# Experts of a mixture: gate and up products as three products of f16 parts, with weights scaled and split one expert ahead

## What is computed

```python
cap = max(1, EC_CAPACITY * N // N_EXPERTS)
aff = jax.nn.softmax((xt @ w_router).astype(jnp.float32), axis=-1)
gates, idx = lax.top_k(aff.T, cap)
xs = xt[idx]
h = jax.nn.silu(jnp.einsum('ecd,edf->ecf', xs, w_gate)) * jnp.einsum('ecd,edf->ecf', xs, w_up)
y = jnp.einsum('ecf,efd->ecd', h, w_down) * gates[..., None].astype(x.dtype)
out = jnp.zeros((N, D), x.dtype).at[idx.reshape(-1)].add(y.reshape(-1, D).astype(x.dtype))
```

## Time and profile before

| | us |
|---|---|
| median of 3 runs | 3354.52 |
| lowest, highest | 3351.68, 3358.54 |
| the profiled execution | 3351.22 |
| its span | 3349.4 |

### The profile page before, as it was taken

How to read it: one execution, slowest core, us unless ns; L and a number is a source line. 1 busy time by engine, 2 the same in 40 slices (tenths; PEclk the granted TensorE clock), 3 DMA queues, 4 the chain that set the end, 5 groups by cost and what they waited for, 6 DMA issues and landing times. The chain is left out here.

```text
span 3349.4 us, 39224 instructions
## 1 busy us (share of the span) xinstructions
PE 2938.2 (88%) x14279; PEld 1610.0 (48%) x14279; DVE 1591.5 (48%) x2416; ACT 1308.5 (39%) x2322; POOL 1002.2 (30%) x928
## 2 busy tenths in 40 slices
PE   7999999869999999779868969999009999999998
PEld 4555555535555555423222324454006566566664
DVE  3244444358888888565575543332781111111111
ACT  3333333249999999674345422222001110110100
POOL 0111111148888888650163001111000111111111
PEclk9999999979999999899979979999559999999999
DMA  5112232225111111288858973433403645556551
GB/s 150 40 52 79 79 91 77 68 68 199 33 33 33 33 33 33 67 358 294 282 198 329 308 239 115 134 113 94 161 29 104 188 159 170 161 155 189 168 154 29
DMA packets 245478, 443.73 MB, mean 132 GB/s; under 512 B 54494, under 2 KB 135518, under 8 KB 243616
## 3 DMA queue, kind: packets, MB, share of 16 engines
q1 hardware_dynamic: 187952, 354.89, 31.8%
q0 software_dynamic: 10752, 37.75, 5.4%
q10 hardware_dynamic: 46608, 48.92, 4.5%
HBM read 289.73 MB, written 151.73 MB: 132 GB/s over the span
## 5 line engine op out<-in xcount | busy, mean ns | idle before, releaser
L959 POOL TENSOR_TENSOR at_p<-at_pf,at_p 128x512 f16<-128x512 f32 x424 | 512.8, 1221 | 145.7 <-ACT at_p L1093 122.3
L578 PE MATMUL pj_ps<-pj_xT,pj_wch 128*128 128x512 f32 (+1 forms) x960 | 381.0, 550 | 0.8 <-issue 0.8
L1221 DVE TENSOR_REDUCE at_mxs<-at_pM 128x1 f32<-128x512 f32 x512 | 342.3, 685 | 78.5 <-PE at_pM L1120 67.9
L1092 ACT ACTIVATE at_pf<-at_pS,at_scale 128x512 f32<-128x512 f32 x520 | 358.3, 689 | 39.9 <-PE at_pS L1145 39.8
L1093 ACT ACTIVATE at_p<-at_pS,at_scale 128x512 f16<-128x512 f32 x520 | 355.2, 683 | 0.0
L1164 PEld LDWEIGHTS at_pO<-at_vv,at_p 128*128 128x128 f16 x4160 | 234.2, 98 | 141.0 <-POOL at_p L959 31.9
L2342 ACT ACTIVATE ex_si<-ex_pG 128x288 f32<-128x288 f32 x64 | 26.3, 410 | 660.9 <-PE ex_pG L2369 653.6
L1164 PE MATMUL at_pO<-at_vv,at_p 128*128 128x129 f16 x4160 | 268.3, 207 | 8.3 <-POOL at_p L959 6.4
L2369 PE MATMUL ex_pG<-ex_xT,mo_gate 128*128 128x288 f32 x1024 | 261.9, 410 | 0.6 <-ACT ex_xT L2335 0.6
L578 PEld LDWEIGHTS pj_ps<-pj_xT,pj_wch 128*128 128x128 f32 x960 | 179.4, 190 | 167.7 <-issue 162.4
L2369 PE MATMUL ex_pU<-ex_xT,mo_up 128*128 128x288 f32 x1024 | 258.8, 406 | 0.0
(11 more groups left out here) (240 smaller groups left out, 4251.6 us busy)
## 6 DMA issues: line engine op xcount, KB each, us to landing
sp_rows<-s_F SPq DMA_DIRECT2D x76, 768.0 KB, 6.9
s_F<-fs_a SPq DMA_DIRECT2D x72, 768.0 KB, 4.8
mo_gate<-in_w_gate SPq DMA_DIRECT2D x16, 2048.0 KB, 8.3
mo_up<-in_w_up SPq DMA_DIRECT2D x16, 2048.0 KB, 13.2
mo_down<-in_w_down SPq DMA_DIRECT2D x16, 2048.0 KB, 11.1
s_G<-sp_gg ACTq DMA_DIRECT2D x72, 256.0 KB, 5.8
sp_tab<-tab_spec SPq DMA_DIRECT2D x76, 192.0 KB, 4.5
s_QK<-pj_R ACTq DMA_DIRECT2D x18, 768.0 KB, 4.4
```

Of the source, the lines that this page charges most:

```text
L578: last = pe.matmul(pU[n % 2][:, 0:width], wch[ch % 2][:, k, :], xT[:, k, t0:t0 + width], start=(k == 0), stop=(k == KD - 1))
L959: eng.tensor_tensor(p2[r][:, :], pf[:, r, :], p1[r][:, :], ALU.subtract).then_inc(own_done if n in own else others_done, 1)
L1092: act.activation(pf[:, n % 4, :], pS[n % 2][:, 0:QB], ACT.Exp, scale=scale[:, 0:1])
L1221: dve.tensor_reduce(mxs[:, j // NC, j % NC:j % NC + 1], pM[j % 2][:, :], AX.X, ALU.max).then_inc(pM_free, 1)
```

## The change

Weights: instead of two f32 buffers for gate and for up there is one f32 buffer `raw` (both), and two buffers each of `hi` and `lo`, f16. The weights of an expert are multiplied by a scale, the inverse root of the sum of all squares of gate and up times 2^15 (the sums divided by 2^30 first); `hi` is that in f16, `lo` the rest in f16. The tokens get a scale from the norm gain `mlp_norm` and are split the same way into `xT` and `xL`. A product is then hi·xT + hi·xL + lo·xT. ScalarE's silu and VectorE's product take the inverse scale `back`.

The work per expert, done for e + 1 during step e: ScalarE squares four parts of `raw`, two after its silu of f = 1 and two after f = 2 (`hi` takes the squares, which nobody reads; the sums count); PE adds the sums over partitions with a matrix of ones, behind its last up product and ahead of `turn`; ScalarE moves the result behind its copies; GpSimd makes the scale, behind its gather; ScalarE makes four parts of `hi`; VectorE makes four parts of `lo`, one behind each of the four ys. `raw` of e + 2 is loaded when the last `lo` part of e + 1 is made. The down weights and their loads stay as they were. For expert 0 the same is done in `choose`, with GpSimd's subtractions in place of VectorE's. PE now turns slice k + 2 when VectorE has made `xL` of slice k.

```diff
-def load_gate_up(eng, io, weights, e, b):
-    for name in ("gate", "up"):
-        eng.dma_start(weights[name][b][:, :, :], io["w_" + name][0, e, :, :].rearrange("(k p) f -> p k f", p=P)
-                      ).then_inc(weights["gu_in"][b], 16)
+def load_gate_up(eng, io, weights, e):
+    for g, name in enumerate(("gate", "up")):
+        eng.dma_start(weights["raw"][:, g, :, :], io["w_" + name][0, e, :, :].rearrange("(k p) f -> p k f", p=P)
+                      ).then_inc(weights["raw_in"], 16)
+def square_part(act, weights, e, b, i):
+    if i == 0:
+        act.wait_ge(weights["raw_in"], 32 * e + 32)
...
+    act.activation(part_of(weights["hi"][b], i), part_of(weights["raw"], i), ACT.Square, scale=1 / MOST,
+                   accum_out=weights["sums"][:, i:i + 1]).then_inc(weights["squared"], 1)
+def add_squares(pe, weights, out, e):
+    pe.wait_ge(weights["squared"], W_PARTS * e + W_PARTS)
...
+    for i in range(W_PARTS):
+        last = pe.matmul(out, weights["ones"][:, :], weights["sums"][:, i:i + 1], start=(i == 0), stop=(i == W_PARTS - 1))
+    last.then_inc(weights["summed"], 1)
+def find_scale(pool, weights, e, b):
...
+    pool.tensor_tensor(size[:, 1:2], size[:, 0:1], tiny[:, 0:1], ALU.add).then_inc(weights["floored"], 1)
...
+    pool.tensor_tensor(weights["scale"][b][:, :], size[:, 1:2], tiny[:, 1:2], ALU.pow).then_inc(weights["powered"], 1)
+def make_hi(act, weights, e, b, i):
...
+    act.activation(part_of(weights["hi"][b], i), part_of(weights["raw"], i), ACT.Copy, scale=weights["scale"][b][:, 0:1]
+                   ).then_inc(weights["hi_made"], 1)
+def make_lo(eng, weights, e, b, i):
+    eng.wait_ge(weights["hi_made"], W_PARTS * e + i + 1)
+    eng.scalar_tensor_tensor(part_of(weights["lo"][b], i), part_of(weights["raw"], i), weights["scale"][b][:, 0:1],
+                             part_of(weights["hi"][b], i), ALU.mult, ALU.subtract).then_inc(weights["lo_made"], 1)
...
-                sp.wait_ge(up_made, FT * e + FT)
-                load_gate_up(sp, io, weights, e + 2, b)
+                sp.wait_ge(weights["lo_made"], W_PARTS * e + 2 * W_PARTS)
+                load_gate_up(sp, io, weights, e + 2)
...
                 if more:
                     gather(e + 1, 1 - b)
+                    find_scale(pool, weights, e + 1, 1 - b)
...
+                    if more and f in (1, 2):
+                        for i in (2 * f - 2, 2 * f - 1):
+                            square_part(act, weights, e + 1, 1 - b, i)
                 if more:
                     copies(e + 1, 1 - b)
+                    act.wait_ge(x_low, KD * e + 2 * KD)
+                    move_size(act, weights, pN, e + 1)
+                    for i in range(W_PARTS):
+                        make_hi(act, weights, e + 1, 1 - b, i)
...
-                        pe.wait_ge(xT_ready, KD * e + k - 1)
+                        pe.wait_ge(x_low, KD * e + k - 1)
...
-                            last = pe.matmul(out[f % 2][:, 0:NTOK], w[b][:, k, f * P:(f + 1) * P], xT[:, k, :],
-                                             start=(k == 0), stop=(k == KD - 1))
+                            for w, x in ((hi, xT), (hi, xL), (lo, xT)):
+                                last = pe.matmul(out[f % 2][:, 0:NTOK], w[b][:, g, k, f * P:(f + 1) * P], x[:, k, :],
+                                                 start=(k == 0 and w is hi and x is xT), stop=(k == KD - 1 and w is lo))
                         last.then_inc(done, 1)
+                if more:
+                    add_squares(pe, weights, pN, e + 1)
...
+                if more:
+                    leave_x(e + 1)
+                    find_back(e + 1, 1 - b)
...
                         dve.tensor_scalar(ys[b][c][0:n, half], pY[0:n, half], now_w[b][0:n, c:c + 1], None, ALU.mult
                                           ).then_inc(y_ready, 1)
+                        if more:
+                            make_lo(dve, weights, e + 1, 1 - b, 2 * c + h)
```

More of the change, by code:

```diff
@@ L2070, in moe @@
         sem = semaphores(nc, ctx, "mo_")
-        weights = {name: [ctx.enter_context(nc.sbuf_tensor(f"mo_{name}{b}", shape, F32)) for b in range(2)]
-                   for name, shape in (("gate", [P, KD, FE]), ("up", [P, KD, FE]), ("down", [P, FE // P, D]))}
-        weights["gu_in"] = [sem(f"gu_in{b}") for b in range(2)]
+        weights = {"raw": ctx.enter_context(nc.sbuf_tensor("mo_raw", [P, 2, KD, FE], F32)),
+                   "sums": ctx.enter_context(nc.sbuf_tensor("mo_sums", [P, W_PARTS], F32)),
+                   "ones": ctx.enter_context(nc.sbuf_tensor("mo_ones", [P, P], F32)),
+                   "tiny": ctx.enter_context(nc.sbuf_tensor("mo_tiny", [P, 2], F32)),
+                   "size": ctx.enter_context(nc.sbuf_tensor("mo_size", [P, 4], F32)),
+                   "x_scale": ctx.enter_context(nc.sbuf_tensor("mo_x_scale", [P, 1], F32))}
@@ L2074, in moe @@
+        for name, shape, dt in (("down", [P, FE // P, D], F32), ("hi", [P, 2, KD, FE], F16), ("lo", [P, 2, KD, FE], F16),
+                                ("scale", [P, 1], F32)):
+            weights[name] = [ctx.enter_context(nc.sbuf_tensor(f"mo_{name}{b}", shape, dt)) for b in range(2)]
         weights["d_in"] = [sem(f"d_in{b}") for b in range(2)]
+        for name in ("raw_in", "squared", "summed", "sized", "floored", "powered", "hi_made", "lo_made", "x_sized"):
+            weights[name] = sem(name)
@@ new lines, in part_of @@
+def part_of(w, i):
+    g, half = divmod(i, 2)
+    return w[:, g, half * KD // 2:(half + 1) * KD // 2, :]
+def square_part(act, weights, e, b, i):
+    if i == 0:
+        act.wait_ge(weights["raw_in"], 32 * e + 32)
+        if not (isinstance(e, int) and e == 0):
+            act.wait_ge(weights["summed"], e)
+    act.activation(part_of(weights["hi"][b], i), part_of(weights["raw"], i), ACT.Square, scale=1 / MOST,
+                   accum_out=weights["sums"][:, i:i + 1]).then_inc(weights["squared"], 1)
@@ new lines, in find_scale @@
+def find_scale(pool, weights, e, b):
+    size, tiny = weights["size"], weights["tiny"]
+    pool.wait_ge(weights["sized"], e + 1)
+    if not (isinstance(e, int) and e == 0):
+        pool.wait_ge(weights["powered"], e)
+    pool.tensor_tensor(size[:, 1:2], size[:, 0:1], tiny[:, 0:1], ALU.add).then_inc(weights["floored"], 1)
+    pool.wait_ge(weights["floored"], e + 1)
+    if not early(e):
+        pool.wait_ge(weights["lo_made"], W_PARTS * (e - 1))
+    pool.tensor_tensor(weights["scale"][b][:, :], size[:, 1:2], tiny[:, 1:2], ALU.pow).then_inc(weights["powered"], 1)
@@ L2114, in choose @@
         idx = sb("idx", [2 * E_N, NTOK], U32)
+        gain, squares = sb("gain", [P, D]), sb("squares", [P, D], BF16)
         lists = sb("lists", [2 * E_N, 4, NC * P])
@@ L2146, in _ @@
             last.then_inc(back, 1)
+            pe.wait_ge(consts, 3)
+            add_squares(pe, weights, pN[:, 0:1], 0)
             pe.wait_ge(listed, 4)
@@ L2159, in _ @@
             act.activation(aff[:, 0:HALF[0]], pA[:, 0:HALF[0]], ACT.Copy).then_inc(aff_ready, 1)
+            act.wait_ge(gain_in, 16)
+            act.activation(squares[:, :], gain[:, :], ACT.Square, scale=D ** 0.5 / MOST, accum_out=weights["size"][:, 2:3]
+                           ).then_inc(weights["x_sized"], 1)
+            for i in range(W_PARTS):
+                square_part(act, weights, 0, 0, i)
+            move_size(act, weights, pN[:, 0:1], 0)
+            for i in range(W_PARTS):
+                make_hi(act, weights, 0, 0, i)
+            act.wait_ge(weights["hi_made"], W_PARTS)
+            for i in range(W_PARTS):
+                raw = part_of(weights["raw"], i)
+                act.activation(raw, raw, ACT.Copy, scale=weights["scale"][0][:, 0:1]).then_inc(raw_scaled, 1)
             act.wait_ge(columns, 1)
@@ L2238, in experts @@
         eye = sb("eye", [P, P])
-        wg, wu, wd = weights["gate"], weights["up"], weights["down"]
+        hi, lo, wd = weights["hi"], weights["lo"], weights["down"]
+        x_scale, scale = weights["x_scale"], weights["scale"]
         now_g = [sb(f"now_g{b}", [P, NC], I32) for b in range(2)]
@@ L2431, in step @@
                         if c == 2:
-                            dve.tensor_scalar(part[0:n, half], pY[n * h:n * h + n, half], now_w[b][0:n, c:c + 1], None, ALU.mult
+                            if h or not (isinstance(e, int) and e == 0):
+                                dve.wait_ge(y_ready, 2 * NC * e + 2 * c + h)
+                            dve.tensor_scalar(part[0:n, :], pY[n * h:n * h + n, half], now_w[b][0:n, c:c + 1], None, ALU.mult
                                               ).then_inc(halved, 1)
```

101 lines of the change are left out of this document (85 added, 16 removed).

## The result

The changed kernel takes 3389.87 us (median of 4 runs, 3388.37 to 3393.85) against 3354.73 (4 runs, 3351.68 to 3358.54): ratio 1.0109, 95% interval 1.0093 to 1.0125. It is slower by 35 us. The profiled execution took 3393.85 us, its span is 3392.1, 42.7 more than before.

The account below looks back on a forecast made before the run. PE was taken as the bound, at 51.60 us an expert. Experts 1 to 14 +77, expert 0 -1.7, expert 15 -7.2, first turning and products +3.4: +71.5 on 3351.2 gives 3422 us, range 3360 to 3455.

Parts of the forecast that it names:

- the sum: Forecast for each of experts 1 to 14, added from its steps: 57.1 us against 51.6 before.
- up weights landed: Raw weights' load, slowed by scatters and gather, lands 20.9 us after the expert's first gate product starts (S).
- landing to the last square: On ScalarE behind the load: two squares, a silu, two squares and small waits, 8.2 us.
- PE idle ahead of L2121: After gate and up, PE waits for ScalarE's squares before the products adding their sums: 5.3 us.
- tiny products: PE's small f32 products adding up the squares' sums, ahead of the turning: 1.2 us.
- turning: PE transposing the next expert's tokens, with VectorE as third hand: 6.1 us, 8.0 at half clock.
- Y to the next S: Start of down products to the next expert's first gate product: 16.7 us plus 2.1 lost to half clock.
- rival (c): Only scatters delay the raw load, gather comes behind: landing S + 17.3; 3372 us, 13%; with full clock 3316, 3%.
- rival (b): PE's clock stays up in the experts though the rest is right: 3367 us; chance 9%.
- Rival (a): Raw load lands early and the kernel is faster: 3322 us with a clock fall, 3293 without; chance 11%.
- Rival (d): Sample scatter waits for all loads in flight, next gather lands past S + 33: 3478 us; chance 4%.
- Rival (e): Gate and up f16 products slower than 124 ns; up to 151 ns they cost nothing; no chance given.

Follow-up runs that it names:

- e5: Changed kernel, with only an eighth of the gate and up weights loaded from expert 2 on, all other work the same: 3316.24 us.
- e3: Changed kernel, with 20 idle products on PE in the wait for the squares and one behind each turned slice: 3353.41 us.
- e7: Changed kernel, with the raw load in four parts and one idle product of 512 columns behind each turned slice: 3286.15 us.
- e1: Changed kernel, with the raw weights loaded in four parts, each as soon as its low part is made: 3315.38 us.
- e4: Changed kernel, with only a quarter of each part of the weights squared, loads as they were: 3342.31 us.
- e2: Changed kernel, with the product lo * xT left out, so 128 instead of 192 products an expert: 3376.44 us.
- e10: e7, with the fourth low part of the weights made behind the sample tokens' operations instead of ahead of them: 3344.3 us.
- e9: e1, with no low part of the tokens made by VectorE and hi * xT computed twice instead: 3263.16 us.

## Why the prediction was right, and where its sizes were off

The direction, the place and the chain of the mechanism (late load, squares, PE's wait, fallen clock) were right, the size too large: +71 us forecast, +43 on the span and +35 on the median measured. Step by step, for a typical expert of 54.4 us against the 57.1 of the sum:

| term | forecast | measured |
|---|---|---|
| up weights landed | S + 20.9 | S + 18.4 |
| landing to the last square | 8.2 | 8.1 |
| PE idle ahead of L2121 | 5.3 | 2.8 |
| tiny products | 1.2 | 1.8 |
| turning | 8.0 | 7.3 |
| Y to the next S | 18.8 | 18.8 |

**The landing** is the term that was mis-sized, by 2.5 us. The issue was right (S + 1.0 against 1.3 for the up half). The load took 17.4 - 13.2 = 4.2 us more than alone, where 2.8 were read from the down load for the scatters. The queue of scatters and gather had the engines for 3.6 us of it; the other 0.6 us, and whether the down load right behind has a part in them, stay open. The gather, which the sum charged with 3.6, costs next to nothing in eleven of fourteen experts, because its first packets come just when the load is through; in the other three the landing was S + 20.4 to 22.0, near the forecast. I had put the gather's traffic at the 1.7 us behind its issue that it had before; here 4.4 lie between, and e5 (1.8 with an eighth of the load) shows that the load makes the difference. So in eleven experts not the forecast's own path came about but that of rival (c) with a fallen clock (the gather comes behind), which had 13% and S + 17.3; with 4.2 in place of 2.8 us it gives S + 18.7, against 18.2 to 18.9 measured. The two errors have opposite signs, 3.6 too much and 1.4 too little, and the time lies between the two forecasts, 3372 and 3422. What was not seen either is how sharp the edge is: in expert 14 the gather's packets came 0.8 us earlier than in the typical expert, and the load landed 3.6 us later.

**The clock** fell in each of the 14 experts (13.7 us at 0.50 in most), as forecast; rival (b) is out. Its price came in other places: the tiny products run at half clock (1.8 instead of 0.9 us), the turning loses 0.9 instead of 1.9 us, since three hands in turn hide most of PE's slowness (1.77 us for two slices at half clock, 1.52 at full in e3 and e7, idle products included), and the down products lose the 2.1. Together 3.9 us from the rows, 4.1 by e3; forecast were 4.0. The page TensorE: Matmul & The Clock Gate of the Trainium skill (HAM oscillation — how this bites in real kernels) says of a wait ahead of each tile of a loop that the clock's fall is paid at every tile; the trace agrees, 14 times, here with a wait of 2.8 us in the typical expert. But e1 shows the clock fall also without the pause, behind the tiny products and in the turning, which the forecast didn't separate.

**Rival (a)**, faster by an early load, was the true potential: the break-even at S + 15.4 that the forecast named lies 3 us from what was measured, and e1 passes it. **Rival (d)** stayed out as a cause, though the gather's landing at S + 25.2 in e4 shows it was next in line. The Trainium skill's page DMA: Bandwidth & Descriptors (Queues, rings and completion order) has each engine take turns between queues packet by packet; the queue rows of expert 14, 66% and 37%, agree. The forecast also called (c) weak by it, and there the runs speak otherwise: with the load ahead of it the gather's first packet came 4.4 instead of 1.7 us after its issue, and eleven experts went the way of (c). **Rival (e)** held: 122 ns, and e2 shows that even fewer products would give nothing in experts 1 to 14.

**The ends**: expert 0 -1.5 (forecast -1.7), expert 15 -7.4 (-7.2). The agreement of expert 0 is in part luck: it took 51.3 us where 49.9 were put, and the kernel before took 52.9 where the sum had 51.6; in both it begins at half clock, for about 3 us, which the sum left out. The first turning and what goes ahead of it were +4.8 instead of +3.4, a term that the sum gives without its parts; as the earlier trace rows now read:

```profile
2510.75 0.66 PE L2493 MATMUL ex_pT<-ex_eye,ex_xs 128*128 128x128 f32 x2 [13.01 <-DMA ex_xs<-s_XN,ex_now_g]
...
2519.20 0.42 PE L2508 MATMUL ex_pG<-ex_xT,mo_hi 128*128 128x288 f16 x1 [1.09 <-DVE ex_xL L2562]
```

The turning itself takes 8.4 instead of 5.7 us there, and it starts 2.1 later; what delays the start wasn't tested. It may be scatter: in e2, e3 and e5, whose work up to there is that of the changed kernel, the first S lies at 2517.3, 2520.7 and 2516.6 us.

**The durations** taken from other forms held: squares, scalings and low parts were put at 1.92, 1.92 and 2.35 us.

```profile
L2154 DVE SCALAR_TENSOR_TENSOR mo_lo<-mo_raw,mo_scale,mo_hi 128x2048 f16<-128x2048 f32 x60 | 140.5, 2342 | 0.0
L2148 ACT ACTIVATE mo_hi<-mo_raw,mo_scale 128x2048 f16<-128x2048 f32 x60 | 115.2, 1990 | 15.8 <-POOL mo_scale L2141 15.8
L2112 ACT ACTIVATE mo_hi<-mo_raw 128x2048 f16<-128x2048 f32 x60 | 113.9, 1899 | 135.8 <-DMA mo_raw<-in_w_up 135.8
```

Open: how much of the clock's price the pause alone brings, and how much the turning, isn't settled in the changed kernel itself, since no run filled the one without the other. With the load in parts and so without the pause the fallen clock costs 49.5 - 47.3 = 2.2 us an expert (e1, e7), with the pause 4.1 (e3): by this estimate, made across two forms of the kernel, about half.

## What to carry to other kernels

When an engine's work is made cheaper, ask first when the buffer that feeds the new steps comes free: here one buffer, emptied by the last of four steps, moved a load by 20 us and took the whole gain of 7 us an expert, and loading each quarter as it came free gave the gain back. A pause on TensorE can cost more than its length: 2.5 us among dense products cost another 1.7 us in clock in eleven of fourteen experts of e10, and nothing in three. One idle product behind each turned slice was cheaper here than the fall: 29 us less in e7 than in e1. A transfer's price beside others depends on whether its packets overlap in time: look at the first packet, not at the issue.

## What the runs showed of the hardware that was not expected

GpSimd's mark of 128x1, the tick ahead of each scatter and ahead of the gathers, took 189 ns in the mean before and 1112 after:

```profile
L2296 POOL TENSOR_TENSOR ex_mark<-ex_mark 128x1 f32<-128x1 f32 x64 | 12.1, 189 | 671.8 <-DVE ex_ys L2439 446.9
...
L2415 POOL TENSOR_TENSOR ex_mark<-ex_mark 128x1 f32<-128x1 f32 x64 | 71.1, 1112 | 332.2 <-DVE ex_ys L2606 145.2
```

It is long where VectorE's low part runs beside it. First GpSimd, then VectorE, in the changed kernel:

```profile
3060.64 2.14 POOL L2415 TENSOR_TENSOR ex_mark<-ex_mark 128x1 f32<-128x1 f32 x1 [2.90 <-DVE ex_ys L2606]
...
3065.97 0.18 POOL L2415 TENSOR_TENSOR ex_mark<-ex_mark 128x1 f32<-128x1 f32 x1 [1.45 <-DVE ex_ys L2602]
```

```profile
3060.39 2.34 DVE L2154 SCALAR_TENSOR_TENSOR mo_lo<-mo_raw,mo_scale,mo_hi 128x2048 f16<-128x2048 f32 x1
```

The mark starts in the low part and ends with it, and the scatter is issued 3.2 us behind the start of the last ys. e10 moves the low part and the long mark moves with it. The second prompt scatter's mark is short again, and the scatter is issued 1.6 us behind the start of the last ys, as in the kernel before; that is 1.6 us earlier than in the changed kernel, where about 2 were expected. The sample scatter's mark is long now, as the low part (2676.45 to 2678.78) lies beside it, so the rival (the mark is long because of the scatter ahead of it) falls:

```profile
2671.51 0.18 POOL L2420 TENSOR_TENSOR ex_mark<-ex_mark 128x1 f32<-128x1 f32 x1 [2.90 <-DVE ex_ys L2619]
...
2676.70 2.14 POOL L2420 TENSOR_TENSOR ex_mark<-ex_mark 128x1 f32<-128x1 f32 x1 [2.94 <-DVE ex_ys L2615]
```

The Trainium skill's GPSIMD Engine Reference (1. Specifications) says that GpSimd shares its SBUF interfaces with VectorE and contends with VectorE instructions that have two inputs in SBUF; the rows agree: a tiny operation that takes 0.18 us alone lasts 2.14 us, to the end of VectorE's.

The other surprise is that in e1 the clock falls in the turning, with no pause ahead of it, where it did not in the kernel before. VectorE as the third hand is a part of it but not all: in e9, with two hands again, the clock still fell in five of fourteen experts, for 3.4 instead of 6.8 us. What differs there from the kernel before are the tiny products ahead of the turning and a turning of 4.3 instead of 3.7 us; which of them does it wasn't tested. One product of 512 columns behind each slice keeps the clock at 1.00 in all fourteen experts of e7.
